# Two-block transformer kernel on one core: the layer-0 input columns and both output projections computed as three products of split halves

## What is computed

```python
def first_block(x, mem, ...):
    mem_n = rms_norm(mem, mem_norm)
    for i in range(2):
        h = rms_norm(x, norm_pre_mix[i])
        if i == 0:
            proj = h @ w_in_a[0]          # q, k, v, gate: 4 x 768 columns, and a few more
            mix = gated_deltanet(proj[..., :IN_A - X_WIDTH], ...)
            mem_q = proj[..., IN_A - X_WIDTH:]
        else:
            proj = h @ w_in_b[0]
            mix = stick_breaking_attention(q, k, v)
            mem_q = proj[..., 3 * W:]
        cross = memory_attention(mem_q, mem_n @ w_mem_kv[i])
        y = concatenate([mix, cross], axis=-1) @ w_out[i]      # 1024 x 1024
        x = x + rms_norm(y, norm_post_mix[i])
        h = rms_norm(x, norm_pre_mlp[i])
        y = square(relu(h @ w_up[i])) @ w_down[i]
        x = x + rms_norm(y, norm_post_mlp[i])
    return x
```

## Time and profile before

| | |
|---|---|
| median of 3 runs | 3725.37 us (3724.54 to 3730.91) |
| the profiled execution | 3726.93 us |
| its span, first to last instruction | 3725.2 us |
| granted PE clock, mean | 0.960 of full speed |
| PE busy | 3307.7 us (89%) |
| DVE, POOL, ACT busy | 2218.0, 1880.4, 699.3 us |
| input columns of layer 0 on PE | 76.7 to 292.0 us, with cross attention, keys and values between |
| output projection of layer 0 on PE | 472.4 to 527.7 us |
| output projection of layer 1 on PE | 1229.8 to 1284.8 us |

### The profile page before, as it was taken

The page is one execution under the profiler, slowest core; times in us unless marked ns, Lnnn a source line. Parts: engine busy times, 40 slices in busy tenths (PEclk is TensorE's granted clock), DMA queues, the critical chain, the costliest instruction groups (busy, mean ns, idle before and its releaser), DMA issues.

```text
span 3725.2 us, 34171 instructions
## 1 busy us (share of the span) xinstructions
PE 3307.7 (89%) x12251; PEld 2124.7 (57%) x12251; DVE 2218.0 (60%) x4206; ACT 699.3 (19%) x1419; POOL 1880.4 (50%) x1174
## 2 busy tenths in 40 slices
PE   8999989998978999989999889789998777777776
PEld 5548848886845488867877667544444233333332
DVE  3655543335543333358935677777777778777775
ACT  2442231112125211121112331101001101011000
POOL 1122229885410298878877448244344434444442
PEclk9999999999979999999999998999999999999999
DMA  3441012322410123232432202699999999999997
GB/s 117 135 137 45 1 53 95 101 90 90 145 59 1 45 91 102 90 101 80 139 111 75 75 29 93 238 404 412 409 417 399 422 421 422 422 419 414 411 418 325
DMA packets 276710, 749.92 MB, mean 201 GB/s; under 512 B 13129, under 2 KB 203090, under 8 KB 211026
## 3 DMA queue, kind: packets, MB, share of 16 engines
q0 software_dynamic: 73728, 536.90, 34.9%
q1 hardware_dynamic: 198624, 204.53, 17.3%
q10 hardware_dynamic: 4210, 6.56, 0.5%
HBM read 739.56 MB, written 8.39 MB: 201 GB/s over the span
## 4 chain that ended last, share of the span: by engine, by line
PE 64%; DMA 19%; DVE 11%; issue 3%; ACT 2%; POOL 1%; ACTq 0%; DVEq 0%; POOLq 0%; SPq 0%
DMA arena<-in_peer_uv,rstd 15%; PE bank L1104 10%; PE bank L1105 10%; PE bank L1106 10%; PE bank L1569 8%; PE bank L1022 8%; DMA normed<-in_peer_uv,rstd 2%; DMA weight_ring<-in_peer_uv,rstd 2%; PE bank L1495 1%; PE bank L1513 1%; PE bank L1388 1%; PE bank L1583 1%; DVE arena L2780 1%; PE bank L1277 1%; PE bank L1416 1%
## 5 line engine op out<-in xcount | busy, mean ns | idle before, releaser
L908 POOL TENSOR_TENSOR split_arena<-weight_ring,ones 128x1024 fp32r<-128x1024 f32 x218 | 537.6, 2466 | 592.4 <-PE bank L1022 321.4
L968 POOL DMA_INDIRECT arena<-in_peer_uv,rstd x419 | 470.1, 1122 | 672.5 <-PE bank L1569 605.9
L1106 PE MATMUL bank<-split_arena 128*128 128x512 f32 x1744 | 686.1, 393 | 0.0
L2780 DVE CUSTOM_DVE_ANT_0 arena<-arena,branch 128x1024 f32<-128x1024 f32 x419 | 512.7, 1225 | 272.0 <-DMA arena<-in_peer_uv,rstd 269.7
L910 POOL TENSOR_TENSOR split_arena<-weight_ring,split_arena 128x1024 fp32r<-128x1024 f32 x218 | 557.2, 2556 | 17.1
L1569 PE MATMUL bank<-arena,level_mask 128*128 128x512 f32 x840 | 414.8, 638 | 125.8 <-DVE level_mask L2762 125.6
L1569 PE MATMUL bank<-arena,row_diagonals 128*128 128x512 f32 x836 | 392.4, 612 | 74.5 <-DVE row_diagonals L2762 74.4
L1104 PE MATMUL bank<-split_arena 128*128 128x512 f32 x1072 | 421.4, 393 | 21.5 <-DVE split_arena L2184 14.0
L1105 PE MATMUL bank<-split_arena 128*128 128x512 f32 x1072 | 418.7, 391 | 0.0
L1106 PEld LDWEIGHTS bank<-split_arena 128*128 128x128 f32 x1744 | 329.6, 189 | 72.1
L1569 PEld LDWEIGHTS bank<-arena,level_mask 128*128 128x128 f32 x840 | 161.5, 201 | 366.5 <-DVE level_mask L2762 194.6
(11 more groups left out here) (425 smaller groups left out, 4837.5 us busy)
## 6 DMA issues: line engine op xcount, KB each, us to landing
weight_ring<-in_w_up SPq DMA_DIRECT2D x32, 1024.0 KB, 5.4
weight_ring<-in_w_down SPq DMA_DIRECT2D x32, 1024.0 KB, 5.0
weight_ring<-in_w_in SPq DMA_DIRECT2D x32, 1024.0 KB, 5.8
weight_ring<-in_ada_w SPq DMA_DIRECT2D x24, 1024.0 KB, 7.7
weight_ring<-in_peer_wq SPq DMA_DIRECT2D x16, 1024.0 KB, 22.1
weight_ring<-in_w_in_a SPq DMA_DIRECT2D x13, 1024.0 KB, 5.2
weight_ring<-in_w_out SPq DMA_DIRECT2D x12, 1024.0 KB, 7.3
weight_ring<-in_w_in_b SPq DMA_DIRECT2D x10, 1024.0 KB, 6.9
```

The costliest lines, as they stand in the source:

```text
L908: pool.tensor_tensor(hi, part, bc_mid(ones[:], DT), ALU.mult).then_inc(split_hi, 1)
L968: pool.indirect_dma_start(row_slots[slot_of[r]], None, a["peer_uv"], bass.IndirectOffsetOnAxis(ap=experts[n % 2][:, c:c + 1], axis=0)).the ...
L1106: return pe.matmul(psum[t.bank][:], hi, a_lo[:, k, :], start=False, stop=k == DT - 1)
L2780: dve.tensor_tensor_reduce(row, row, h_tok[:, r // NE, :], 1.0, 0.0, ALU.mult, ALU.add, dots[:, i % 4, j:j + 1]).then_inc(dot_ready, 1)
```

## The change

`qkv_units` and both sets of `out_units` get the split way. Their high weight parts are made by ACT (`high_half`, one 128 x 1024 copy per half), the low parts by POOL (`low_half`). Three slots hold the parts, so ACT writes half i+3 once half i is done. The inputs are split too: ACT copies the high part of each of 8 tiles, DVE subtracts (8 in layer 0's entry, 8 for each output projection). The output projections start with two tiles side by side and take the two cross-attention tiles first (`MIX_ORDER`). A ring slot of such a unit is free when its low parts are made, not when PE is done.

```diff
@@ POOL
+            def low_half(u, h, w):
+                hi, lo = [x.rearrange("p (k n) -> p k n", n=P) for x in w(u.split + h)]
+                pool.wait_ge(high_ready, u.high + h + 1)
+                pool.tensor_tensor(lo, raw(u)[:, :, h * P:(h + 1) * P], f32(hi), ALU.subtract).then_inc(split_ready, 1)
...
-            for u in ada_units:
-                if u.layer == 0:
-                    pool.wait_ge(landed[u.slot], 16 * u.load)
-                    pool.tensor_tensor(raw(u), raw(u), bc_last(c_col[:], UNIT_N), ALU.mult).then_inc(mod_scaled, 1)
+            for j, u in enumerate(qkv_units):
+                if j == LH:
+                    for x in kv_units[1]:
+                        scale_modulation(x.then)
+                for h in range(2):
+                    low_half(u, h, column_w)
+                scale_modulation(u.then)
...
+                for u in out_units[l]:
+                    for h in range(2):
+                        low_half(u, h, branch_ws[l])
@@ PE
-                if i % 2 == 0:
-                    pe.wait_ge(landed[u.slot], 16 * u.load)
-                product(u, i % 2, t, normed_x)
+                pe.wait_ge(split_ready, u.split + i % 2 + 1)
+                free(pe, t)
+                split_product(u, i % 2, column_w, t, high_in[0], each(split_H),
+                              (lambda k: pe.wait_ge(in_split, k + 1)) if i == 0 else None)
...
-            project(out_units[0], out_tiles[0], mixed_in, ready=mixed(0))
-            total_sum(post[0], branch_sq)
+            split_out(0)
...
-            project(out_units[1], out_tiles[1], mixed_in, ready=mixed(1))
-            total_sum(post[1], branch_sq)
+            split_out(1)
@@ ACT
+            def high_half(u, h, w):
+                hi, _ = [x.rearrange("p (k n) -> p k n", n=P) for x in w(u.split + h)]
+                act.wait_ge(landed[u.slot], 16 * u.load)
+                act.activation(hi, raw(u)[:, :, h * P:(h + 1) * P], ACT.Copy).then_inc(high_ready, 1)
...
                 if 1 <= i <= 3 * LH and i != 2 * LH:
                     silu(i - 1)
+                if i + 3 < 4 * LH and not 2 * LH <= i + 3 < 2 * LH + 3:
+                    column_high(i + 3)
...
+            for t in scan[TT - 1]["o"]:
+                have(act, t)
+            high_half(out_units[0][1], 0, column_w)
...
+            cross_high(0)
+            head_scale(o_sums, 2 * LH, q_f, 1.0 / P, tail=mixed_tail)
+            branch_out(0)
...
                     take(x, Y[:, k, :])
+                    if k + 3 < DT:
+                        high_half(out_units[l][(k + 3) // 2], (k + 3) % 2, branch_ws[l])
@@ DVE
+            def mixed_low(l, k):
+                at = MIX_ORDER.index(k)
+                dve.wait_ge(in_high, IN_OUT[l] + at + 1)
+                dve.tensor_tensor(low_in[k], mixed_in[k], f32(high_in[l][k]), ALU.subtract).then_inc(in_split, 1)
...
+            full(dve, head_tile)
+            for k in range(DT):
+                dve.wait_ge(in_high, k + 1)
+                dve.tensor_tensor(split_H[:, k, :], H[:, k, :], f32(high_in[0][k]), ALU.subtract).then_inc(in_split, 1)
```

More of the change, by code:

```diff
@@ L82, in __init__ @@
         self.slot, self.load, self.before = slot, load, before
-        self.then, self.split = None, None
+        self.then, self.split, self.own, self.high = None, None, None, None
 def build(nc, a, out):
@@ L929, in _ @@
                 split_half(u, h, wide_w, ((landed[u.slot], 16 * u.load),
-                                          (half_done, 2 * wide_units[0].u + (back if i >= 4 else -back))), u.split + h + 1)
+                                          (half_done, 2 * wide_units[0].u + (back if i >= 4 else -back))), u.own + h + 1)
             pool.wait_ge(half_done, 2 * (wide_units[-1].u + 1))
@@ L955, in _ @@
                          (half_done, 2 * ya_units[0].u + i + 1 - OUT_SLOTS))
-                split_half(u, h, out_w, ((landed[u.slot], 16 * u.load), place), u.split + h + 1)
+                split_half(u, h, out_w, ((landed[u.slot], 16 * u.load), place), u.own + h + 1)
             for r in range(NROW):
@@ L1108, in split_product @@
-            def split_product(u, h, w, t, a_hi, a_lo, ready):
-                for k in range(DT):
-                    ready(k)
-                    m = split_steps(u.split + h, w, t, a_hi, a_lo, k)
+                pe.matmul(psum[t.bank][:], hi, a_hi[k], start=first, stop=False)
+                pe.matmul(psum[t.bank][:], lo, a_hi[k], start=False, stop=False)
+                return pe.matmul(psum[t.bank][:], hi, a_lo[k], start=False, stop=last)
+            def split_product(u, h, w, t, a_hi, a_lo, ready=None, order=range(DT)):
+                for i, k in enumerate(order):
+                    if ready:
+                        ready(i)
+                    m = split_steps(u.split + h, w, t, a_hi, a_lo, k, i == 0, i == DT - 1)
@@ L1113, in split_product, with split_first @@
                 m.then_inc(half_done, 1)
-            def split_first(us, w, tiles, a_hi, a_lo, ready):
-                for k in range(DT):
-                    ready(k)
+            def split_first(us, w, tiles, a_hi, a_lo, ready, order=range(DT)):
+                for i, k in enumerate(order):
+                    ready(i)
                     for j, t in enumerate(tiles):
-                        if k == 0:
+                        if i == 0:
                             pe.wait_ge(split_ready, us[0].split + j + 1)
@@ L1146, in ready @@
                                     pe.wait_ge(up_ready, i * QT + (FT * l + k + 1))
-                            split_product(u, h, mlp_w, t, a_hi, a_lo, ready)
+                            split_product(u, h, mlp_w, t, each(a_hi), each(a_lo), ready)
                 quarter(0, 3)
@@ L1901, in logs, with stick_high @@
                     act.activation(w, w, ACT.Ln, bias=1.0).then_inc(zabs_ready, 1)
+            def stick_high(k):
+                for h in (2 * k, 2 * k + 1):
+                    have(act, stick[h]["out"])
+                out_high(1, k)
             logs(0)
@@ L2400, in _ @@
                         m.then_inc(bank_out[t.bank], 1)
+            for k in range(MT, DT):
+                mixed_low(0, k)
             for h in range(LH):
@@ L2428, in _ @@
             cross_attention(1)
+            for k in range(MT, DT):
+                mixed_low(1, k)
             dve.wait_ge(lb_exp, 2)
```

161 lines of the change are left out of this document (115 added, 46 removed).

## The result

The changed kernel takes **3693.5 us** (median of four runs, 3691.0 to 3701.0) against 3726.9 us (four runs, 3724.5 to 3730.9) for the kernel before on the same chip: 33.5 us less, a ratio of 0.9913 with a 95% interval of 0.9895 to 0.9930. The forecast was 3681, its range 3672 to 3695: the direction and the range held, the gain was smaller than the 44.5 us forecast. The profiled execution took 3691.0 us with a span of 3689.3, 35.9 less than the span before. It is the fastest of the four; its mean granted clock is 0.959 (0.960 before; 0.954 to 0.955 in the other three), so the two profiles can be compared stretch by stretch.

A forecast was written before the change was run, and what follows sets the result against it. PE was taken to bound the input columns, with POOL and ACT having room. 57.1 - 2.3 - 1.0 - 3.9 - 5.4 = 44.5 us gained gave 3681 us, range 3672 to 3695; gain 34 to 50 at 70%.

The forecast's parts named there:

- The gain per tile: Input columns and both projections: a split tile takes 5.44 us instead of 6.87, 1.43 less, 57.1 us in all.
- The parts that were costed at nothing: ACT's high copies, POOL's low parts and the input splits: hidden in idle time or slack, cost 0.
- The rival with three slots as the pace: Low parts come late, so PE waits on every tile; at L = 18 plus 38 us, 3763; slower given 2%.
- The lock in the cross heads: DVE's normalization held by POOL's operations: first head 1.8 us, third 0.5, two and four 0; 2.3 us, bounds 0 and 14.4.
- The sign that the prediction named: A DVE normalization of 2 to 3 us beside the first cross head, with PE idle behind it.
- Before tile 12: Input columns: the unit's late load makes PE wait for its low part; 1.0 us lost, between 0.3 and 4.6.
- The head loop: Layer 0: extra ACT copies ahead of and inside the loop start PE's output projection 3.9 us later, bounds 2.2 to 5.
- more seams open: Rival: ACT's queue or a clock fall in the head loop, and twice the lock; gain 22 to 34, about 3697; 11%.
- The projection behind the loop: Layer 0's output projection: 8 split tiles, each 1.43 us less, gain 11.4 us.
- The tails: After each projection's last output tile: POOL's later fourth MLP half holds DVE 2.7 us longer; 5.4 us for two layers.
- Layer 1's projection: Layer 1's output projection to its MLP: 8.7 us gained, from 11.4 for its tiles and 2.7 lost after them.
- ACT's queue: Cause within a rival: ACT's in-order queue, where a high part waits for its load while the exponentials stand behind it.

The follow-up runs named there:

- run 7: Changed kernel, but ACT makes the high part of input half i+2, not i+3, after tile i; 3706.1 us, ratio 0.9947.
- run 1: Changed kernel, but three of POOL's scalings wait until DVE has normalized cross heads one, three and four; layer 1's key scaling does not wait; 3688.6 us.
- run 2: Changed kernel, but the negation of the row maxima (128x2) moves from DVE to ACT, POOL left as it is; 3688.8 us.
- run 10: The changed kernel unaltered, measured again beside two edited versions on one chip; 3694.4 us, ratio 0.9921.
- run 9: Changed kernel with layer 1's output projection plain again, no high, low or input parts there; 3697.8 us, ratio 0.9931.
- run 8: Changed kernel with cross high parts before the scan, weight half 2 after the head loop, and POOL, not ACT, copying the six mixed tiles; 3694.8 us.
- run 3: Changed kernel, but POOL starts each layer's fourth MLP half only when all eight MLP inputs are split; 3687.0 us, ratio 0.9898.
- run 11: Changed kernel with two holds on POOL: scalings after the normalized heads, fourth MLP half after the split inputs; 3680.1 us, ratio 0.9874.

## Why the prediction held, and where it was off

**The gain per tile** (57.1 us in all): right. Split tiles start 5.44 us apart, in the columns and in both projections. The parts that were costed at nothing cost nothing: ACT's copies of 128 x 1024 take 1.06 us (1.04 counted), the input splits hide, and the low parts come in time even with one slot's lead less (run 7). The rival with three slots as the pace was far off. Only around the turns and the modulation products is a tile's gain 1.38 to 1.40 instead of 1.43, about 1 us in 24 tiles.

**The lock in the cross heads** (2.3 us): the mechanism was right, the term mis-sized, and this is most of the error. PE waits 7.8 us there, and a half-clock spell adds 1.4 us. The step that failed is "the normalization of a cross head is" such an operation: I had looked only for DVE operations with two SBUF inputs and passed over the one with one input and 128 x 2 elements in front of it. So I expected the scaling to be met at its end: in run 1 the normalization is due 1.4 us before the point where the scaling ended (89.20 and 90.58). The negation meets it 2.9 us before that point. And head four was counted at 0, though a key's scaling waits for its load until just then. The sign that the prediction named, a normalization of 2 to 3 us beside the first head, did not come (1.23). Run 1 gives 8.2 us back, run 2 shows both forms held.

**Before tile 12** (1.0): 0.3 more wait than before, inside the bounds.

**The head loop** (3.9): the copies and the pace took what was counted, and run 10, like runs 7 and 9, measures 3.9. In the first profile it is 4.9, inside the bound of 5: the sums of the first two heads took 1.4 us more there, at the lower clock, of which 1.0 reaches the end of the loop. The prediction has such a fall only in the rival "more seams open". Where the sums of the later heads run at half clock (2.05 us for 1.10) nothing is lost, because ACT's turn of 2.3 us covers them. The projection behind the loop gains 1.0 less than counted; its first tile takes 6.4 us, layer 1's 5.6. In run 8, with the copies off ACT, no sum ran at half clock.

**The tails** (2 x 2.7): 2.83 and 2.81. Both operations were held, as priced. Run 3 shows that the mechanism was already costing 1.4 us a tail before the change.

**Layer 1's projection** (8.7): 8.5 in place, shown twice, by the change and by its undoing.

**The rest**: the delta stage and scan lost 1.7 us and the stretch up to layer 1's projection gained 2.4. Both hold work of the change (high and low parts for the next projection), but both move by as much between the profiles of experiments that leave them as they are in the changed kernel: 169.2 to 172.5 us for the first, where runs 2, 3 and 7 have the 169.2 to 169.3 of the kernel before, and 687.9 to 694.1 for the second. The sum made against one profiled execution: 44.5 forecast, 35.9 measured, 8.6 less. The heads took 6.9 more than their term, the tiles around the turns about 1, the head loop 1.0, the projection behind it 1.0, the delta stage 1.7; the stretch up to layer 1's projection gave 2.4 back, tile 12 cost 0.7 less than counted, and the rest is small.

That the range held is in part luck. The medians gain 33.5 us, half a us below the 34 at which the forecast's 70% ended and the rival "more seams open" (22 to 34, 11%) began, and two of that rival's three causes did come: the hold in the heads cost over three times its term, and the clock fell in the head loop, though the fall cost 1 to 2 us and not 3. The third, ACT's queue, did not (run 1).

The Trainium skill (SBUF — State Buffer, Who interferes with whom) has more than the rule on two inputs that I went by: it also lists `tensor_scalar` among the DVE operations that can enter a mode with two ports and then contend with GpSimd. The trace agrees, with 0.17 us turned into 2.93, 3.31 and 3.56, the rest of the POOL operation each time; that part of the rule, applied to the negation, would have led to this term. Who follows when both wait, which I left open, run 8 shows for its one pattern: POOL, waiting behind DVE's low part, goes before DVE's next scale.

## What to carry to other kernels

When work moves to POOL, list every DVE operation between SBUF and SBUF on the path, however small, and see which POOL operation it will meet; a tiny one early in a chain costs as much as a large one. Then hold POOL's long operations that nobody needs yet behind a semaphore of that chain: two such waits brought 14 us here, nearly half of what the change itself did. Hold every one that can meet the chain: where one stays free, a tenth of a us decides who goes first (head four in runs 1 and 11). Price a step by its stretch in the trace, and do not expect a 3 us stretch to show in a median when the granted clock varies between executions.

## What the hardware showed that I had not expected

- An operation on only 128 x 2 numbers is held as long as a large one (3.56 us instead of 0.17); the convolution, which reads one input from PSUM and writes there, is not: 0.754 us mean over 42 of them in run 1's columns, with POOL at work beside them.
- The hold goes both ways: POOL's 128 x 512 copy took 1.27 us where DVE was idle at its start and 1.67 behind DVE's low part (run 8).
- Executions of one kernel differ with the mean granted clock. Over the 91 executions of this study, each against its own kernel's mean, 0.001 of clock goes with 1.8 us: run 3's kernel took 3676.4 us at 0.961 and 3690.5 at 0.955. The changed kernel averages 0.956 in nine executions, the kernel before 0.9605 in 31; by that slope, which is one within kernels and need not hold between two, the change would have gained some 8 us more at an equal clock (an estimate). Whether the new waits cause it or only go with it is open, except in the input columns, where runs 1 and 7 show it falling after them.
